# Value products of the decode tile in a two-mixer encoder layer: 64-column stationaries for the two heads of a pair, and one take-out of y

## The reference, cut to what matters

```python
def sb_attend(q_pos, q, k, v, k_pos):
    z = jnp.einsum('bhqd,bhkd->bhqk', q, k) * (HEAD_DIM ** -0.5)
    mask = k_pos[None, :] < q_pos[:, None]
    log_skip = jnp.where(mask, jax.nn.log_sigmoid(-z), 0.0)
    later = lax.cumsum(log_skip, axis=3, reverse=True) - log_skip
    w = jnp.where(mask, jnp.exp(jax.nn.log_sigmoid(z) + later), 0.0)
    return jnp.einsum('bhqk,bhkd->bhqd', w, v)

def fox_attend(q_pos, q, fq, k, v, k_pos, fk):
    z = ... + fq[..., :, None] - fk[..., None, :]
    p = jax.nn.softmax(jnp.where(k_pos[None, :] <= q_pos[:, None], z, -jnp.inf), axis=-1)
    return jnp.einsum('bhqk,bhkd->bhqd', p, v)
```

## Time and profile before

| | us |
|---|---|
| median of 3 runs | 1643.24 |
| lowest, highest run | 1642.31, 1644.11 |
| span of the profiled execution | 1643.0 |
| TensorE matmuls busy | 1497.1 (91%) |
| TensorE weight loads busy | 1317.2 (80%) |
| VectorE busy | 927.6 (56%) |
| ScalarE busy | 747.6 (46%) |
| products of line 1117, with their loads | 14.9 and 15.6 |

### The profile page before, as it was taken

One profiled execution on the slowest core, in us unless ns is written; L12 is line 12 of the kernel. 1 busy time (PEld: TensorE's weight loads), 2 busy tenths in 40 slices (PEclk: granted clock), 3 DMA queues, 4 the chain that ended last, 5 costly groups with the idle time before them and its releaser, 6 DMA issues. The chain is left out here.

```text
span 1643.0 us, 23239 instructions
## 1 busy us (share of the span) xinstructions
PE 1497.1 (91%) x8603; PEld 1317.2 (80%) x8603; DVE 927.6 (56%) x1182; ACT 747.6 (46%) x1074; POOL 167.1 (10%) x125
## 2 busy tenths in 40 slices
PE   6899999999999989888999999989986998999950
PEld 3589899999999988777899999968845876788840
DVE  6622112223323228888766745442256997999958
ACT  8522111213332227776666731131115776777733
POOL 0000000000000010000000001111101323334320
PEclk9899999999999999999999999989987999999985
DMA  8265454548666648575678424454346899999465
GB/s 297 77 167 181 121 142 152 160 142 229 213 210 196 184 122 210 153 179 131 149 175 189 115 91 132 151 179 144 115 178 217 246 334 287 280 275 287 104 166 227
DMA packets 231898, 300.03 MB, mean 183 GB/s; under 512 B 86333, under 2 KB 171429, under 8 KB 231778
## 3 DMA queue, kind: packets, MB, share of 16 engines
q1 hardware_dynamic: 222282, 263.94, 53.6%
q0 software_dynamic: 9504, 34.61, 8.7%
HBM read 264.16 MB, written 87.81 MB: 214 GB/s over the span
## 5 line engine op out<-in xcount | busy, mean ns | idle before, releaser
L751 PE MATMUL G<-hhi,proj_whi 128*128 128x384 f32 x768 | 178.0, 339 | 0.0
L751 PE MATMUL G<-hhi,proj_wlo 128*128 128x384 f32 x768 | 175.6, 336 | 0.0
L751 PE MATMUL G<-hlo,proj_whi 128*128 128x384 f32 x768 | 175.6, 336 | 0.0
L2125 DVE TENSOR_TENSOR experts_ulo<-plain,experts_uhi 128x2048 fp32r<-128x2048 f32 (+1 forms) x68 | 151.2, 2225 | 16.6 <-ACT experts_uhi L2062 14.2
L1110 PE MATMUL G<-items_WT,items_vt 128*128 128x128 f32 x1152 | 151.6, 277 | 1.6 <-DMA items_vc<-in_cache_sb_v_dram 1.6
L1110 PEld LDWEIGHTS G<-items_WT,items_vt 128*128 128x128 f32 x1152 | 142.3, 192 | 2.4 <-DMA items_vc<-in_cache_sb_v_dram 1.8
L751 PEld LDWEIGHTS G<-hhi,proj_whi 128*128 128x128 f32 x768 | 135.8, 188 | 2.4 <-DVE proj_wlo L831 2.0
L751 PEld LDWEIGHTS G<-hhi,proj_wlo 128*128 128x128 f32 x768 | 137.5, 188 | 0.0
L751 PEld LDWEIGHTS G<-hlo,proj_whi 128*128 128x128 f32 x768 | 137.5, 187 | 0.0
L2062 ACT ACTIVATE experts_uhi<-plain 128x2048 fp32r (+1 forms) x68 | 126.5, 1865 | 17.2 <-PE G L2018 7.4
L2018 PE MATMUL G<-experts_uhi,experts_ghi 128*128 128x512 f32 x264 | 109.9, 416 | 8.1 <-DVE experts_glo L2130 6.7
(11 more groups left out here) (337 smaller groups left out, 3004.0 us busy)
## 6 DMA issues: line engine op xcount, KB each, us to landing
plain<-in_w_dram SPq DMA_DIRECT2D x132, 512.0 KB
plain<-in_w_dram SPq DMA_DIRECT2D x33, 1024.0 KB
proj_wraw<-in_w_ada_dram SPq DMA_DIRECT2D x24, 512.0 KB
proj_wraw<-in_w_in_dram SPq DMA_DIRECT2D x20, 512.0 KB
qkhi_d<-proj_ohi SPq DMA_DIRECT2D x16, 576.0 KB, 2.8
qklo_d<-proj_olo SPq DMA_DIRECT2D x16, 576.0 KB, 3.0
gate_d<-proj_full SPq DMA_DIRECT2D x15, 576.0 KB, 2.9
pre_raw<-in_w_ada_dram SPq DMA_DIRECT2D x16, 512.0 KB, 5.6
```

The source lines that it names most:

```text
L751: m = pe.matmul(G[:, g + c, 0:CH], w[r][:, k, :], a[:, k, c * CH:(c + 1) * CH], start=k == 0 and q == 0, stop=k == KD - 1 and q == 2)
L2125: dve.tensor_tensor(half(ulo[j], c)[:, part, :], raw_up(side[n], c)[:, part, :], half(uhi[j], c)[:, part, :].bitcast(F32), ALU.subtract).t ...
```

## The change

For the sample tile each head gets products of its own: the stationary operand is the 64 channels of that head, and the output goes to partitions 0 to 63 (even head) or 64 to 127 (odd head), both in columns 0 to 127. The two heads' products alternate. There are 2 products of 128 columns in place of one of 256, and 16 of 16 columns in place of 8 of 32. Since y of both heads now stands in the same columns, `high_y` and `low_y` take it in one operation of 128 partitions each, and the semaphores count one instead of two.

```diff
-                y_parts = [2 if paired(n) else 1 for n in range(NI) if y_last(n)]
-                y_done = [sum(y_parts[:y]) for y in range(len(y_parts) + 1)]
+                rows_of = lambda n: slice(0, P) if late(n) else slice(items[n][1] % 2 * HD, (items[n][1] % 2 + 1) * HD)
...
                         if t % 4 == 0 and y >= 2:
-                            pe.wait_ge(y_lo, y_done[y - 1])
+                            pe.wait_ge(y_lo, y - 1)
...
-                            out = G[:, 4 + y % 2, 0:2 * P]
-                            pe.matmul(out, vt[v][:, TT - 1, :], W2[v][:, 1].rearrange("p e n -> p (e n)"), start=True, stop=False)
-                            pair = out.rearrange("p (e n) -> p e n", e=2)
+                            side_of = [slice(e * HD, (e + 1) * HD) for e in both]
+                            for e in both:
+                                pe.matmul(G[side_of[e], 4 + y % 2, 0:P], vt[v][:, TT - 1, side_of[e]], W2[v][:, 1, e, :], start=True, stop=False)
                             for b in range(NB):
-                                new = slice(b * NQ, (b + 1) * NQ)
-                                m = pe.matmul(pair[:, :, new], vc[v][:, b, :], W2[v][:, 0, :, new], start=False, stop=b == NB - 1)
+                                for e in both:
+                                    new = slice(b * NQ, (b + 1) * NQ)
+                                    m = pe.matmul(G[side_of[e], 4 + y % 2, new], vc[v][:, b, side_of[e]], W2[v][:, 0, e, new], start=False, stop=b == NB - 1)
                         m.then_inc(pv_done, 1)
...
-                        for e in both if late(n) else (h % 2,):
-                            a, t0, w = slice(e * HD, (e + 1) * HD), t // 4 * 4, (t % 4 + 1) * P
-                            first = e * P if late(n) else 0
-                            act.activation(yhi[a, 4 * f + h // 2, t0 * P:t0 * P + w], G[a, 4 + y_use(n) % 2, first:first + w], ACT.Copy).then_inc(y_hi, 1)
+                        a, t0, w = rows_of(n), t // 4 * 4, (t % 4 + 1) * P
+                        act.activation(yhi[a, 4 * f + h // 2, t0 * P:t0 * P + w], G[a, 4 + y_use(n) % 2, 0:w], ACT.Copy).then_inc(y_hi, 1)
...
-                        dve.wait_ge(y_hi, y_done[y_use(n) + 1])
...
+                        dve.wait_ge(y_hi, y_use(n) + 1)
+                        a, t0, w = rows_of(n), t // 4 * 4, (t % 4 + 1) * P
+                        dve.tensor_tensor(ylo[a, c, t0 * P:t0 * P + w], G[a, 4 + y_use(n) % 2, 0:w],
+                                          yhi[a, c, t0 * P:t0 * P + w].bitcast(F32), ALU.subtract).then_inc(y_lo, 1)
```

## The result

| | before | after |
|---|---|---|
| median, us | 1643.67 | 1634.93 |
| lowest, highest run | 1642.31, 1644.11 | 1633.86, 1635.86 |
| span of the profiled execution | 1643.0 | 1634.1 |

The changed kernel is faster by 8.7 us: ratio 0.9945, 95% interval [0.9933, 0.9957]. A second set of five runs, beside the experiments, gave 0.9951 [0.9935, 0.9968]. Forecast were 1637.6 us and a range of 1634 to 1645, so the direction and the mechanism held and the gain was undersized: 5.6 forecast, 8.7 measured.

What follows compares the result with a forecast made beforehand. TensorE was taken to bound the forgetting half, TensorE and VectorE by turns the stick-breaking half. Gains 2.25 + 2.75 + 0.6 = 5.6 us gave 1643.2 - 5.6 = 1637.6 us, range 1634 to 1645.

Steps and rivals of the forecast that it cites:

- What bounds: Attention stage: TensorE bounds the forgetting half, busy 22.00 of 22 us a head; in stick-breaking TensorE 19.5, VectorE 18.8.
- Halves side by side: Sample products' block: loads for the array's two halves overlap, 1.58 us in place of 2.13, -0.55 a block; chance 0.50.
- the four larger: Sample block's four records with 64-column loads and 128 moving columns, put at 0.30 us of the block.
- The change of form at nothing: Sample block: going from full array to narrower stationary and back costs nothing, up to 0.05 us for each of 16.
- Part 2: y taken out in one operation: 0.58 us a block behind three stick-breaking blocks, nothing in the forgetting half.
- the ceiling: Behind each stick-breaking block: VectorE's own product for the 512-column item limits the gain to 0.75 us at most.
- The end of the stage: After the last small product: one y operation each on ScalarE and VectorE saves 0.6 us, once.
- The clock behind the seam: Behind the stage's end: shorter TensorE idle time may prevent the clock's fall, 1.7 us more gain; chance 0.3 within each case.
- the sum's own formula: Gain = 3 x min(0.58 - s, 0.75) + 5 x (-s) + 0.6, s the block's change; total 5.6 us.
- Rival 1: Sample block: loads stay one after another, +0.10 us a block, gain 1.5 us, 1641.7 us; chance 0.33.
- Rival 2: Sample block: each change of half stalls the load, +1.5 us a block, 1652.9 us; chance 0.15.

Runs made afterwards that it cites:

- The take-out alone: Kernel before, products unchanged, with y taken out in one operation and the odd heads' part of the sample's y not computed: 1639.6 us, ratio 0.9971.
- split tiles and quarters: Changed kernel with prompt value products of tiles 4 to 7 split between array halves, and sample products cut into four 32-column stationaries: 1624.1 us, ratio 0.9879.
- its twin with earlier loads: The kernel just named, with the next pair's values loaded a head sooner: 1623.6 us with split tiles and quarters, 1622.0 us with tiles 4 to 7 split.
- tiles 4 to 7 split: Changed kernel with the prompt's value products split between array halves for tiles 4 to 7 of each head only: 1617.9 us, ratio 0.9841.
- products in a row: Changed kernel with the 16 small products in two runs, all even head then all odd head, instead of alternating: 1638.8 us, ratio 0.9972.
- the two with extra full products: Changed kernel, small products overwriting, with four extra full-array products a block, all at the end (1642.4 us) or one behind each two requests (1649.4 us).

## Why the prediction was right, and what it missed

1. **What bounds.** Right. The forgetting half pays every microsecond of TensorE: its four pieces gave 0.76 us each, for blocks 0.87 us shorter and entered 0.08 later (0.40 behind the last score product, before 0.32). The take-out alone gave 0.01 us there.
2. **Halves side by side.** Right, and shown by the alternation's removal (0.027 to 0.051 us a record). **The size was the main miss of the forecast**: the small records had been put at 0.040 us, with an offset between the halves of 10 to 30 ns. The measured 0.027 is half of a half's own step of 0.051, with no offset between the halves to be seen. That is 32 x 0.013 = 0.42 us less; the four larger took 0.27 where 0.30 was forecast, and 0.13 went the other way, the return to the full array behind the last record: 1.58 forecast, 1.26 measured.
3. **The change of form at nothing.** Wrong: 0.21 us a visit. The small records erred the other way, so the block's total doesn't show it. The rows were from a stationary of 41 columns; the prediction said "if those are such changes" and still costed them at nothing.
4. **Part 2.** The place was right everywhere, the ceiling's position too. Its size was 0.75 forecast, 0.97 measured behind the first block, since one operation in place of two saves 0.44 us of VectorE and not 0.30, a step that the trace of the kernel before already showed. Over the three pairs 2.25 forecast, 2.76 measured; by pair 1.00, 0.76 and 1.00. Why the second gives less is open; with one take-out alone it is also 0.24 less (0.85, 0.61, 0.83).
5. **The end of the stage.** Forecast 0.6 for the take-out: 0.61, by two kernels. The last block itself gave 0.97 there, not 0.55.
6. **The clock behind the seam** was a rival with 0.3: the fall did not come in either of the two profiled executions of the changed kernel, and 1.7 of the 8.7 us hang on that. **The reason given, a shorter idle time, falls.** With 2.18 us of idle time and two take-outs the clock stayed at 1.00, with 1.56 us and the take-out alone it was 0.79. The kernel with split tiles and quarters and its twin with earlier loads have the same block and the same 2.08 us of idle time, and one shows 0.79 and the other 1.00:

```profile
942.37:950.37 8.00, 8.00 (x37) 8.00 (x38) 1.38 (x2) 1.26 (x2) 0.00 (x0) 0.79 0.85 263
```

```profile
942.06:950.06 8.00, 8.00 (x46) 8.00 (x47) 2.58 (x3) 1.26 (x2) 0.00 (x0) 1.00 0.88 289
```

The same holds for the kernel with tiles 4 to 7 split and its twin with earlier loads, both with a block of 1.26 us and 1.87 us of idle time: 1.00 and 0.79. So what these runs show is that neither the idle time nor the block decides it alone; what does is open. The changed kernel's gain by its own work is nearer to 7 us, and that the other 1.7 came was luck. A tendency is there: the five kernels with a block of 1.98 us or more (the one before, products in a row, take-out alone, the two with extra full products) all fell, of the nine other profiled executions two did.

By the sum's own formula with the measured sizes, 2.76 + 3.03 + 1.58 = 7.4, and 1.7 for the clock: 9.1, against 8.9 in the spans. The forecast of 5.6 was short by 1.8 in the sizes of points 2, 4 and 5, and by the clock.

Rival 1 (one load after another) came out as the kernel with the products in a row: forecast for it 1641.7, measured 1638.8. Its block was 1.98 us, not the 2.23 of the forecast, and the take-out was undersized for it too. Rival 2 (a stall at each change of half) did not show in any run.

## What to carry to other kernels

Where a stationary is used for 64 of its 128 columns, and loads set the pace, give each half its own products and alternate them: the step between records fell from 0.112 to 0.051 us by the columns and to 0.027 by working side by side, for twice as many records. Count the visits to the halves, since each cost 0.21 us here, and put enough products into one. And look at what waits next: in the stick-breaking half, where VectorE was next in line, fusing two small evictions was worth more than the products (2.29 against 1.33 us by itself), in the forgetting half nothing (0.01 against 2.93).

## What the runs showed of the hardware that was not expected

- Records of narrow products for different parts of the array start 0.027 us apart in halves of 64 columns and 0.009 us in quarters of 32, with float32 operands; in one half alone 0.051 us.
- A visit to the halves costs 0.21 us of TensorE, departure and return together.
- ScalarE and VectorE can write 64 partitions from the other 64 of PSUM; 64x256 by ScalarE took 0.38 us and by VectorE 0.42 us, which is what made the split of the prompt's products possible.
- Two executions whose block and idle time before the seam are the same (2.08 us of idle time in one pair of kernels, 1.87 in another) can differ in the granted clock behind it, 0.79 and 1.00.
- TensorE stopped for 1.17 and 0.75 us inside a row of products without a wait in the code, in the two kernels with quarters and split tiles; why is open.
